# A threshold search on two engines: GpSimd answers ScalarE's count before VectorE's

## The chip, the cores and the metric

The kernel runs on one core of a Trainium2 chip. The metric is the device time of one launch in microseconds (us), where lower is better. Five engines with their own instruction queues work side by side and wait for each other through semaphores: TensorE (PE, with PEld for its weight loads), VectorE (DVE), ScalarE (ACT), GpSimd (POOL) and SyncE (SP, which only issues DMAs here).

## The reference, cut to what matters

One decoder layer is computed for a prompt of 2048 tokens and for 8 x 4 sample tokens: an input projection, a convolution branch, a sparse attention branch, and a mixture of experts. The change touches the prompt's sparse attention alone. There an indexer scores every earlier token for every query, the 256 best are kept, and attention runs over those:

```python
def indexer_select(qi, wi, kidx, qpos, k_sel):
    dots = jnp.einsum('bqhd,bsd->bqhs', qi, kidx) * (IDX_DIM ** -0.5)
    score = jnp.einsum('bqhs,bqh->bqs', jax.nn.relu(dots), wi).astype(jnp.float32)
    kpos = jnp.arange(kidx.shape[1])
    score = jnp.where(kpos[None, None, :] <= qpos[None, :, None], score, -jnp.inf)
    return lax.top_k(score, k_sel)[1]
```

The kernel does not sort. It finds for each query the score that separates the 256 best from the others, by halving an interval 25 times, and turns the result into a mask that is added before the softmax.

## The kernel before, in words

The prompt's 2048 queries are 16 tiles of 128. `attend_prompt` works through them in 64 slots `g`, four for each tile, and each slot does two of the tile's eight heads: scores on PE (L1279), mask and maximum on DVE (`masked`, L1548, then `largest`, L1555), exponential on ACT (`exp`, L1402), transposes on PE (L1296), copies of them on ACT (`keep_turned`, L1380), and the product with the values on PE (L1323). While that goes on, the indexer of eight later tiles (`SEEK`: 14, 15, 12, 13, 10, 11, 8, 9) is put between: dots on PE (L1264), relu on ACT (`keep_relu`, L1371), weighted sums over the heads on DVE (`sums`, L1482 to L1486). The longer a tile, the longer its rows, up to 2048 scores for each query.

The threshold search takes these eight tiles in four pairs. Of a pair `q`, VectorE counts the even one (`count_x`, L1499) and ScalarE the odd one (`count_y`, L1411). In each round `r` an engine reads the whole row of scores once and counts how many lie above the tile's current middle. GpSimd then moves the middle (`narrow`, L1630 to L1636) with two tiny instructions of 128x1, L1634 and L1635, and the engine may count the next round. Its waits are `mid_ready[0]` on VectorE and `mid_ready[1]` on ScalarE, and GpSimd's are `counted[0]` and `counted[1]`. So each tile's search is a chain of count, narrow, count, and GpSimd serves both chains in one fixed order.

Where the counts stand in the queues of VectorE and ScalarE is set by tables. `PACE` gives the number of rounds in a tile's four slots, and `PLACES` the places inside a slot, from 0 to 4. On VectorE (`behind`, L1592 to L1614) place 0 follows `masked(g + 1, 0)`, place 1 follows `masked(g + 1, 1)` and `largest`, places 2 and 3 follow one instruction of `sums` each in the slots that have dots (0 to 15, 24 to 31 and 36 to 43), and place 4 comes last. On ScalarE (L1438 to L1459) place 0 follows the first `keep_turned`, place 1 the second one and the first `keep_relu`, place 2 the first `exp`, place 3 the second `keep_relu` and the second `exp`, and place 4 comes last. The first search runs in slots 8 to 17 (2 or 3 rounds a slot), the second in 22 to 28 and the third in 36 to 43 (up to 5 rounds a slot), the fourth in 46 to 52 (4 rounds a slot). Since each engine's queue is in order, a count that waits for its middle holds up everything behind it.

GpSimd has little else to do here: `begin` sets up a pair, `bounds` and `finish` close it, and it issues some gathers when all searches are over.

Of the kernel before, what the change touches and what calls it, by code (L numbers as in the profile page):

```python
# [1159 lines left out]
def attend_prompt(nc, c, early, edges, kT, kiT, v_tok, wi_tok):  # L1160
# [3 lines left out]
    with Phase(nc, "q_") as ph:  # L1164
# [58 lines left out]
        with ph.block() as block:  # L1223
# [30 lines left out]
            def _(pe):  # L1254
                def dots(j, m, chunks):
                    if m == 0:
                        pe.wait_ge(qi_loaded[j % 2], 16 * (j // 2 + 1))
                    for k, (a, b) in list(enumerate(cuts(seek_length(j), 512)))[chunks]:
                        free, _, _ = at.dots[j, m, k]
                        if free:  # L1260
                            pe.wait_ge(s_free[k % 2], free)
                        for x in range(2):
                            rows = slice(x * HD, x * HD + HD)
                            nc.tensor.matmul(ps_s[k % 2][:, 512 * x:512 * x + b - a], qi_st[rows, j % 2, m, :], kiT[rows, a:b],  # L1264
                                             start=True, stop=True).then_inc(s_full[k % 2], 1)

                def scores(g, u):
                    t = g // 4
                    if g % 4 == 0 and u == 0:
                        pe.wait_ge(q_loaded[t % 2], 64 * (t // 2 + 1))  # L1270
                    a, b = cuts(length(t), 1024)[u]
                    for x in range(2):
                        free, _, _ = at.scores[g, u, x]
                        if free:
                            pe.wait_ge(s_free[x], free)
                    for k0, k1 in cuts(b - a, 512):
                        for x in range(2):
                            rows = slice(x * HD, x * HD + HD)
                            m = nc.tensor.matmul(ps_s[x][:, k0:k1], q_st[rows, t % 2, g % 4, :], kT[rows, g % 4 // 2, a + k0:a + k1], start=True, stop=True)  # L1279
                            if k1 == b - a:  # L1280
                                m.then_inc(s_full[x], 1)
# [81 lines left out]
            def _(act):  # L1363
                def keep_relu(j, m, chunks):
                    for k, (a, b) in list(enumerate(cuts(seek_length(j), 512)))[chunks]:
                        _, full, _ = at.dots[j, m, k]
                        half = at.halves[j, m, k // 2]
                        if k % 2 == 0 and half >= 2:
                            act.wait_ge(relu_used, half - 1)
                        act.wait_ge(s_full[k % 2], full)  # L1370
                        nc.scalar.activation(relu[:, half % 2, :, a % 1024:a % 1024 + b - a],  # L1371
                                             ps_s[k % 2][:].rearrange("p (x k) -> p x k", x=2)[:, :, 0:b - a], ACT.Relu, scale=IDX_SCALE).then_inc(s_free[k % 2], 1)
# [248 lines left out]
            def _(pool):  # L1621
                ch = Chain(pool, g_chain)

                def begin(j):
                    pool.wait_ge(range_ready, j + 1)
                    ch.link(nc.gpsimd.tensor_tensor(span[:, j:j + 1], most[:, j:j + 1], least[:, j:j + 1], ALU.subtract))
                    ch.link(nc.gpsimd.tensor_scalar(width[:, j % 4], pow2[:], span[:, j:j + 1], 1e-30, ALU.mult, ALU.add))
                    nc.gpsimd.tensor_tensor(mid[:, j % 4, 0:1], least[:, j:j + 1], width[:, j % 4, 0:1], ALU.add).then_inc(mid_ready[j % 2], 1)

                def narrow(j, r):  # L1630
                    q = j // 2
                    bound, compare = (TOPK - 0.5, ALU.is_ge) if j % 2 == 0 else (seek_length(j) - 2 * TOPK + 0.5, ALU.is_le)
                    pool.wait_ge(counted[j % 2], q * HALVINGS + r + 1)
                    ch.link(nc.gpsimd.tensor_scalar(step[:, j % 2:j % 2 + 1], count[:, j % 4, r:r + 1], bound, width[:, j % 4, r:r + 1], compare, ALU.mult))  # L1634
                    nc.gpsimd.tensor_scalar(mid[:, j % 4, r + 1:r + 2], mid[:, j % 4, r:r + 1], step[:, j % 2:j % 2 + 1], width[:, j % 4, r + 1:r + 2],  # L1635
                                            ALU.add, ALU.subtract).then_inc(mid_ready[j % 2], 1)  # L1636

                def bounds(j):
                    q = j // 2
                    bound, compare = (TOPK - 0.5, ALU.is_ge) if j % 2 == 0 else (seek_length(j) - 2 * TOPK + 0.5, ALU.is_le)  # L1640
                    pool.wait_ge(counted[j % 2], (q + 1) * HALVINGS)
                    ch.link(nc.gpsimd.tensor_scalar(passed[:], count[:, j % 4], bound, None, compare))
                    ch.mark(nc.gpsimd.tensor_scalar(under[:, j % 2, 0:HALVINGS], passed[:], -1.0, HUGE, ALU.add, ALU.mult))
                    ch.link(nc.gpsimd.tensor_scalar(over[:, j % 2, 0:HALVINGS], passed[:], HUGE, None, ALU.mult))
                    ch.mark(nc.gpsimd.tensor_tensor(under[:, j % 2, 0:HALVINGS], under[:, j % 2, 0:HALVINGS], mid[:, j % 4], ALU.add))
                    ch.mark(nc.gpsimd.tensor_copy(under[:, j % 2, HALVINGS:HALVINGS + 1], least[:, j:j + 1]))
                    ch.mark(nc.gpsimd.tensor_copy(over[:, j % 2, HALVINGS:HALVINGS + 1], most[:, j:j + 1]))
                    ch.link(nc.gpsimd.tensor_tensor(over[:, j % 2, 0:HALVINGS], over[:, j % 2, 0:HALVINGS], mid[:, j % 4], ALU.add))
                    pool.sem_inc(bound_ready, 1)

                def finish(j):
                    n = seek_length(j)
                    pool.wait_ge(chosen, j + 1)
                    ch.link(nc.gpsimd.tensor_tensor(sure[:, 0:n], sure[:, 0:n], edge[:, 0:n], ALU.mult))
                    nc.gpsimd.tensor_scalar(sc_row(j)[:, 0:n], sure[:, 0:n], -HUGE, 0.0, ALU.mult, ALU.add).then_inc(mask_ready, 1)
# [7 lines left out]
                for q in range(len(SEEK) // 2):  # L1663
                    for x in range(2):
                        begin(2 * q + x)
                    for r in range(HALVINGS - 1):
                        for x in range(2):
                            narrow(2 * q + x, r)
                    for x in range(2):
                        bounds(2 * q + x)  # L1670
                    for x in range(2):
                        finish(2 * q + x)
# [1960 lines left out]
```

## Time and profile before

| what | value |
|---|---|
| three runs | 2965.82, 2962.16, 2948.20 us (median 2962.16) |
| the profiled execution, its own time | 2951.22 us |
| its span from first to last instruction | 2949.5 us |
| PE, DVE, ACT, POOL busy | 2681.7, 1964.6, 1490.1, 763.5 us |
| share of the span | 91%, 67%, 51%, 26% |
| granted TensorE clock, mean over the span | 0.967 |

The busy share is an average over stages with different limits. The prompt's attention lies between about 950 and 1770 us of the span. In the page's 40 slices of some 74 us each, those are slices 13 to 23, and there DVE and ACT are both at six to nine tenths, PE at eight to nine. No engine is idle for long, and none is full, so in this stage the order in which the engines wait for one another matters. The rest of the kernel, before and after, is not touched.

Below, a group of rows gives the view it comes from. In a timeline a row reads: start in us from the span's start, duration in us, engine, line, operation, what it writes and reads, the shapes, and in brackets for how long the engine was idle before it and who ended that. A count takes two instructions, the pass over the row and a short one that reads the accumulator, and the count is over when the second ends.

### The profile page before, as it was taken

To read this page: it belongs to the slowest core of one execution; us is meant where nothing else is said; L and a number is where in the kernel's file an instruction comes from. 1 tells how busy PE (TensorE), PEld (TensorE's weight loads), DVE (VectorE), ACT (ScalarE), POOL (GpSimd) and SP (SyncE) were. 2 spreads that over 40 slices of the span, in tenths; PEclk is the share of its full clock that TensorE was granted. 3 is DMA by queue.
4 is the path that set the end of the run, shared out by engine and by line. 5 is a ranking of instruction groups with operands and counts; after the bars stand their busy time and mean duration, and the time that the engine had idled before them with its cause. 6 is when DMAs were issued, how large, how long until landed. Compare 5 with 4: busy or idle time off the path is not lost. (4 is left out here: it accounts for less than half of the span.)

```text
span 2949.5 us, 46736 instructions
## 1 busy us (share of the span) xinstructions
PE 2681.7 (91%) x16568; PEld 1712.6 (58%) x16570; DVE 1964.6 (67%) x3027; ACT 1490.1 (51%) x2535; POOL 763.5 (26%) x1012
## 2 busy tenths in 40 slices
PE   8999999999899888878878888899999599999988
PEld 6887878799898344545455565455545333333333
DVE  2499623689962788787787736574443666676658
ACT  2111123359894588687687756421000255566546
POOL 3344432233233033331333413112230000000025
PEclk9999999999999999999999999999999699999999
DMA  3322333124443221300200138644551587777857
GB/s 130 102 95 88 104 114 92 29 72 133 121 137 126 70 68 51 93 8 14 70 8 12 27 110 276 232 139 156 194 182 54 221 325 276 298 282 289 301 204 295
DMA packets 238167, 412.88 MB, mean 140 GB/s; under 512 B 29276, under 2 KB 153436, under 8 KB 229162
## 3 DMA queue, kind: packets, MB, share of 16 engines
q1 hardware_dynamic: 175122, 249.22, 25.7%
q0 software_dynamic: 24464, 86.40, 8.1%
q10 hardware_dynamic: 38416, 75.08, 7.0%
q8 instruction: 100, 1.64, 0.2%
q14 instruction: 65, 0.53, 0.1%
HBM read 317.30 MB, written 97.44 MB: 141 GB/s over the span
## 5 line engine op out<-in xcount | busy, mean ns | idle before, releaser
L471 PE MATMUL p_ps_acc<-p_x_hi,p_w_hi 128*128 128x352 f32 (+2 forms) x1480 | 529.8, 358 | 10.4 <-POOL p_w_lo L398 8.5
L471 PE MATMUL p_ps_acc<-p_x_lo,p_w_hi 128*128 128x352 f32 (+2 forms) x1480 | 520.8, 352 | 0.0
L471 PE MATMUL p_ps_acc<-p_x_hi,p_w_lo 128*128 128x352 f32 (+2 forms) x1480 | 520.1, 351 | 0.0
L471 PEld LDWEIGHTS p_ps_acc<-p_x_hi,p_w_hi 128*128 128x128 f32 (+1 forms) x1480 | 277.4, 187 | 64.4 <-issue 19.0
L471 PEld LDWEIGHTS p_ps_acc<-p_x_lo,p_w_hi 128*128 128x128 f32 (+1 forms) x1480 | 277.8, 188 | 27.8 <-issue 0.5
L471 PEld LDWEIGHTS p_ps_acc<-p_x_hi,p_w_lo 128*128 128x128 f32 (+1 forms) x1480 | 277.4, 187 | 27.3
L3230 PE MATMUL e_ps_G<-g_shared,e_xT 128*32 128x512 f32 x656 | 290.6, 596 | 1.4 <-issue 1.4
L3230 PE MATMUL e_ps_G<-g_late,e_xT 128*32 128x512 f32 x1312 | 291.4, 595 | 0.3 <-issue 0.2
L3230 PE MATMUL e_ps_G<-l_wgu,e_xT 128*32 x656 | 290.5, 596 | 1.0 <-ACT e_xT L3288 1.0
L626 ACT ACTIVATE p_stage<-p_ps_acc,g_cols 128x352 f32<-128x352 f32 (+3 forms) x145 | 88.4, 610 | 334.2 <-PE p_ps_acc L471 334.2
L396 POOL CAST p_w_hi<-g_late 128x1024 fp32r<-128x1024 f32 x74 | 92.4, 1248 | 590.3 <-PE p_ps_acc L471 447.5
L792 DVE SCALAR_TENSOR_TENSOR g_shared<-g_late,p_taps,g_shared 128x1024 f32<-128x1024 f32 x240 | 226.2, 984 | 4.2
L792 DVE SCALAR_TENSOR_TENSOR g_shared<-g_early,p_taps,g_shared 128x1024 f32<-128x1024 f32 x120 | 205.1, 1709 | 4.3
L398 POOL TENSOR_TENSOR p_w_lo<-g_late,p_w_hi 128x1024 fp32r<-128x1024 f32 x74 | 204.6, 2765 | 6.0
L1296 PE MATMUL q_ps_t<-g_ident,q_sm 128*128 128x128 f32 x1088 | 156.5, 288 | 51.9 <-ACT q_pT L1380 34.2
L1279 PE MATMUL q_ps_s<-a_keys,g_late 64*128 64x512 f32 (+3 forms) x640 | 158.2, 603 | 47.7 <-DVE q_top L1548 19.1
L1296 PEld LDWEIGHTS q_ps_t<-g_ident,q_sm 128*128 128x128 f32 x1088 | 122.4, 146 | 116.6 <-issue 63.1
L1402 ACT ACTIVATE q_sm<-q_sm,q_negmax 128x128 f32<-128x128 f32 (+15 forms) x128 | 153.4, 1199 | 56.7 <-DVE q_negmax L1555 55.8
L3230 PEld LDWEIGHTS e_ps_G<-l_wgu,e_xT 128*32 128x32 f32 x656 | 72.3, 110 | 185.8 <-issue 185.6
L1380 ACT COPY q_pT<-q_ps_t 128x512 f32<-128x512 f32 (+3 forms) x320 | 146.2, 533 | 61.0 <-PE q_ps_t L1296 60.1
L3255 PE MATMUL e_ps_Y<-l_wd,e_hT 128*32 x328 | 148.2, 594 | 21.9 <-DVE e_hT L3369 20.3
L2923 POOL DMA_INDIRECT l_rows<-x,l_slot_tok x41 | 39.0, 952 | 475.6 <-PE e_ps_X L3215 450.0
(598 smaller groups left out, 5763.3 us busy)
## 6 DMA issues: line engine op xcount, KB each, us to landing
g_late<-in_w_in_dram SPq DMA_DIRECT2D x72, 512.0 KB, 3.8
l_wgu<-in_w_gate_dram SPq DMA_DIRECT2D x32, 1024.0 KB
l_wgu<-in_w_up_dram SPq DMA_DIRECT2D x32, 1024.0 KB
l_wd<-in_w_down_dram SPq DMA_DIRECT2D x30, 1024.0 KB, 5.5
yb<-e_y ACTq DMA_DIRECT2D x41, 512.0 KB
featT<-p_stage ACTq DMA_DIRECT2D x28, 528.0 KB
featT<-p_stage ACTq DMA_DIRECT2D x28, 512.0 KB
g_late<-featT SPq DMA_DIRECT2D x56, 256.0 KB, 3.1
```

The costliest lines, as they stand in the source:

```text
L396: nc.gpsimd.tensor_copy(w_hi[:, slot], w[:, slot]).then_inc(w_hi_done, 1)
L398: nc.gpsimd.tensor_tensor(w_lo[:, slot], w[:, slot], w_hi[:, slot].bitcast(F32), ALU.subtract).then_inc(w_split[slot], 1)
L471: m = nc.tensor.matmul(acc[slot][tb][0:rows, 0:width], wp[:, slot, k, 0:rows], xp[:, k, at], start=(k == 0 and i == 0), stop=(k == KD - 1 ...
L626: nc.scalar.activation(into[0:rows, tb * width:(tb + 1) * width], acc[slot][tb][0:rows, 0:width], func, bias=c.cols[0:rows, blk:blk + 1]). ...
L792: ch.mark(nc.vector.scalar_tensor_tensor(dst, src, wt, dst, ALU.mult, ALU.add))
L1279: m = nc.tensor.matmul(ps_s[x][:, k0:k1], q_st[rows, t % 2, g % 4, :], kT[rows, g % 4 // 2, a + k0:a + k1], start=True, stop=True)
L1296: m = nc.tensor.transpose(ps_t[n % 3][:, (k - a) * P:(k - a + 1) * P], sm[:, g % 2, x, k * P:(k + 1) * P], c.ident[:])
L1380: nc.scalar.copy(pT[:, x, a:b, :], ps_t[n % 3][:, 0:(b - a) * P].rearrange("p (b q) -> p b q", q=P)).then_inc(t_kept, 1)
L1402: nc.scalar.activation(row, row, ACT.Exp, bias=negmax[:, g % 2, x:x + 1], scale=SM_SCALE, accum_out=total[:, t % 2, g % 4, x:x + 1]).then_ ...
L2923: pool.indirect_dma_start(w.rows[:, j % 2, :], None, c.x1, bass.IndirectOffsetOnAxis(ap=slot_tok[:, j:j + 1], axis=0)).then_inc(w.x_loaded ...
L3230: m = nc.tensor.matmul(pG[slot][tile_of(x), :].rearrange("p (g f) -> p g f", g=2), xT[:, k, tile_of(x)], weights, start=(k == 0), stop=(k ...
L3255: m = nc.tensor.matmul(pY[h][tile_of(x), :], hT[:, k, tile_of(x)], weights, start=(k == 0), stop=(k == 1))
```

## The change

Inside a round the two narrowings change places. Before, GpSimd waits for VectorE's count, narrows its tile, then waits for ScalarE's count and narrows that. Now it waits for ScalarE's count first. The instructions, their number, the tables, and the queues of all other engines stay as they are, and so does the order of `begin`, `bounds` and `finish`.

```diff
                 for q in range(len(SEEK) // 2):
                     for x in range(2):
                         begin(2 * q + x)
                     for r in range(HALVINGS - 1):
-                        for x in range(2):
+                        for x in (1, 0):
                             narrow(2 * q + x, r)
                     for x in range(2):
                         bounds(2 * q + x)
```

This is GpSimd's queue where the first search starts, before the change. The name in brackets is the semaphore, by an older name of its number: `p_x_loaded0` is `counted[0]` (VectorE's count is over), `p_x_loaded1` is `counted[1]` (ScalarE's), and `p_turned` is GpSimd's own chain.

```order
L1634 TENSOR_SCALAR q_step<-q_count,q_width 128x1 [waits p_x_loaded0]
L1635 TENSOR_SCALAR q_mid<-q_mid,q_step,q_width 128x1 [waits p_turned]
L1634 TENSOR_SCALAR q_step<-q_count,q_width 128x1 [waits p_x_loaded1]
L1635 TENSOR_SCALAR q_mid<-q_mid,q_step,q_width 128x1 [waits p_turned]
L1634 TENSOR_SCALAR q_step<-q_count,q_width 128x1 [waits p_x_loaded0]
L1635 TENSOR_SCALAR q_mid<-q_mid,q_step,q_width 128x1 [waits p_turned]
```

And this is the same place with the change:

```order
L1634 TENSOR_SCALAR q_step<-q_count,q_width 128x1 [waits p_x_loaded1]
L1635 TENSOR_SCALAR q_mid<-q_mid,q_step,q_width 128x1 [waits p_turned]
L1634 TENSOR_SCALAR q_step<-q_count,q_width 128x1 [waits p_x_loaded0]
L1635 TENSOR_SCALAR q_mid<-q_mid,q_step,q_width 128x1 [waits p_turned]
L1634 TENSOR_SCALAR q_step<-q_count,q_width 128x1 [waits p_x_loaded1]
L1635 TENSOR_SCALAR q_mid<-q_mid,q_step,q_width 128x1 [waits p_turned]
```

Only the semaphores have changed places; this goes on for 24 rounds in each of the four searches, 96 rounds in all. At the end of a search the last narrowing is now VectorE's, with `bounds` behind it as before:

```order
L1634 TENSOR_SCALAR q_step<-q_count,q_width 128x1 [waits p_x_loaded0]
L1635 TENSOR_SCALAR q_mid<-q_mid,q_step,q_width 128x1 [waits p_turned]
L1642 TENSOR_SCALAR q_passed<-q_count 128x25 [waits p_x_loaded0]
L1643 TENSOR_SCALAR q_under<-q_passed 128x25 [waits p_turned]
L1644 TENSOR_SCALAR q_over<-q_passed 128x25
```

## Rows read from the trace of the kernel before

**Rows 1.** Four searches: stretch, length, busy PE, PEld, DVE, ACT, POOL; clock, DMA, GB/s.

```profile
1044.00:1186.00 142.00, 119.20 (x712) 63.81 (x712) 126.93 (x155) 118.73 (x171) 49.66 (x99) 0.98 0.20 60
1227.00:1347.00 120.00, 94.92 (x672) 55.72 (x670) 99.45 (x138) 102.57 (x142) 41.89 (x100) 0.93 0.10 30
1427.00:1534.00 107.00, 86.90 (x556) 49.65 (x555) 88.32 (x136) 90.52 (x141) 41.02 (x98) 0.94 0.10 28
1575.00:1663.00 88.00, 67.53 (x582) 46.41 (x579) 61.43 (x116) 75.75 (x121) 35.79 (x111) 0.90 0.04 10
```

**Rows 2.** Waits over the whole span: us in total, times, longest one.

```profile
DVE q_edge L1499 <- POOL q_mid L1635: 35.1, 47, 1.0
ACT q_junk_act L1411 <- POOL q_mid L1635: 30.6, 23, 5.8
```

**Rows 3.** ScalarE's counts (L1411) in the first search: idle before them, until whom.

```profile
  POOL q_mid L1635: 12.8, 7
```

**Rows 4.** The same in the second search, then who waited for these counts.

```profile
  POOL q_mid L1635: 6.3, 5
...
  POOL q_step L1634: 19.2, 16
```

**Rows 5.** The same two in the third search.

```profile
  POOL q_mid L1635: 3.8, 5
...
  POOL q_step L1634: 13.9, 12
```

**Rows 6.** ScalarE's counts in the fourth search: idle before them.

```profile
  POOL q_mid L1635: 7.7, 6
```

**Rows 7.** Timeline of slot 41 (third search), places 1 to 4.

```profile
1501.96 0.20 ACT L1411 ACTIVATION_READ_ACCUMULATOR q_junk_act<-g_early,q_mid 128x1 f32 x1
1502.03 1.68 DVE L1499 TENSOR_SCALAR_CACHE_REDUCE q_edge<-g_early,q_mid 128x1408 bf16<-128x1408 f32 x1
...
1502.26 0.30 POOL L1634 TENSOR_SCALAR q_step<-q_count,q_width 128x1 f32<-128x1 f32 x1 [1.36 <-ACT q_junk_act L1411]
...
1503.64 1.28 DVE L1486 SCALAR_TENSOR_TENSOR q_sc<-g_shared,a_wi_tok,q_sc 128x1024 f32<-128x1024 f32 x1
1503.82 1.26 POOL L1634 TENSOR_SCALAR q_step<-q_count,q_width 128x1 f32<-128x1 f32 x1 [0.78 <-DVE q_edge L1499]
...
1508.30 1.68 DVE L1499 TENSOR_SCALAR_CACHE_REDUCE q_edge<-g_early,q_mid 128x1408 bf16<-128x1408 f32 x1 [0.92 <-POOL q_mid L1635]
1509.36 0.20 ACT L1411 ACTIVATION_READ_ACCUMULATOR q_junk_act<-g_early,q_mid 128x1 f32 x1
...
1510.48 1.58 ACT L1411 ACTIVATE q_junk_act<-g_early,q_mid 128x1536 bf16<-128x1536 f32 x1 [0.92 <-POOL q_mid L1635]
```

**Rows 8.** Timeline of slot 40: the relu's wait, and VectorE's wait after place 3.

```profile
1480.43 1.99 PE L1264 MATMUL q_ps_s<-a_keys,g_late 64*128 64x512 f32 x8 [1.83 <-DVE q_top L1548]
...
1481.66 1.94 ACT L1371 ACTIVATE g_shared<-q_ps_s 128x1024 f32<-128x1024 f32 x2 [2.30 <-PE q_ps_s L1264]
...
1491.66 1.23 DVE L1548 CUSTOM_DVE_ANT_0 q_sm<-q_ps_s,g_late 128x1024 f32<-128x1024 f32 x1 [0.98 <-PE q_ps_s L1279]
```

**Rows 9.** Timeline of slots 50 and 51 (fourth search).

```profile
1627.87 1.47 ACT L1402 ACTIVATE q_sm<-q_sm,q_negmax 128x1408 f32<-128x1408 f32 x1 [0.41 <-DVE q_negmax L1555]
...
1630.84 1.36 ACT L1411 ACTIVATE q_junk_act<-q_sc,q_mid 128x1280 bf16<-128x1280 f32 x1 [1.40 <-POOL q_mid L1635]
...
1639.20 0.75 DVE L1548 CUSTOM_DVE_ANT_0 q_sm<-q_ps_s,g_early,q_top 128x512 f32<-128x512 f32 x1 [1.74 <-PE q_ps_s L1279]
```

**Rows 10.** Timeline of slots 10 and 11 (first search).

```profile
1082.49 0.20 ACT L1411 ACTIVATION_READ_ACCUMULATOR q_junk_act<-q_sc,q_mid 128x1 f32 x1
...
1082.52 1.29 DVE L1486 SCALAR_TENSOR_TENSOR g_late<-g_shared,a_wi_tok,g_late 128x1024 f32<-128x1024 f32 x1
...
1084.18 2.21 DVE L1499 TENSOR_SCALAR_CACHE_REDUCE q_edge<-q_sc,q_mid 128x1920 bf16<-128x1920 f32 x1 [0.38 <-POOL q_mid L1635]
...
1096.81 2.00 ACT L1411 ACTIVATE q_junk_act<-q_sc,q_mid 128x2048 bf16<-128x2048 f32 x1 [1.99 <-POOL q_mid L1635]
```

## The prediction, made before the changed kernel had run

> **What bounds the kernel now.** I read the page first, then busy time by stretch, the waits, one line's own waits, and the timeline. The page shows the 91% of PE, but the change lies in the prompt's attention, where the four searches fill 457 us [rows 1]. There DVE is busy 127 of 142, 99 of 120, 88 of 107 and 61 of 88 us, ACT 119, 103, 91 and 76. In the first search VectorE has the least room, in the second and third both have some 15%, and in the fourth ScalarE is nearly full (76 of 88) while VectorE is not. Phases follow one another, so what this stage gains or loses goes to the end of the kernel nearly in full.
>
> The waits say how much can be won at most: VectorE waits 35.1 us for its middle (47 times, never over 1.0), ScalarE 30.6 us (23 times, up to 5.8) [rows 2]. No gain can pass 66 us, and most of VectorE's part is bare latency that the swap doesn't take away.
>
> **What a narrowing costs.** After ScalarE's count in slot 41 ends at 1502.16 (1501.96 + 0.20), its narrowing starts 0.10 later [rows 7]. VectorE's count in place 4 starts 0.92 us after the one before it ended, with nothing between but the narrowing, and so does ScalarE's [rows 7]. So a pair of instructions with its signals takes 0.92, of which some 0.88 is GpSimd's own turn (0.10 to start, 0.78 for the two). An engine that is served second, with both counts over, waits 1.80.
>
> **What the change does to a round.** It depends on which count ends last.
>
> If ScalarE ends first, before the change it waits for VectorE's count, for VectorE's narrowing and then for its own, and now it is served at once. VectorE loses nothing, since GpSimd is through by the time it asks.
>
> If VectorE ends first, before the change it is served at once, and now it waits for ScalarE's count and two narrowings. Its middle comes later by the lag of ScalarE's count plus 0.88. ScalarE gains nothing: its narrowing always came at once, since VectorE's was long over.
>
> GpSimd waited for ScalarE's count 16 times of 24 in the second search [rows 4] and 12 of 24 in the third [rows 5], so there the second case is the common one.
>
> **Second and third search: the loss.** In slot 41 VectorE counted in place 2 from 1502.03. ScalarE's count of place 1 ends at 1502.16, so now VectorE starts at 1502.16 + 1.80 = 1503.96, that is 1.9 later. Two places on, ScalarE's count of place 3 ends at 1509.56, VectorE may start at 1511.36 where it did at 1508.30: 3.1 later. These are not added up, for the lateness is measured each time against ScalarE, which goes on as before. A slot of four or five rounds thus ends some 3 us later on VectorE.
>
> Does that reach ScalarE? In slot 40 PE waited 1.83 us for VectorE's masked maximum before it did the dots, and ScalarE 2.30 us for those dots before its relu [rows 8]. The relu stands ahead of ScalarE's count of place 1. So the lateness comes back to ScalarE in the next slot, its lag behind VectorE is restored, and VectorE is made late again: it is paid per slot. The slots of this kind are 24 to 27 and 40 to 42, seven of 3 us, 21 us. Against it stands idle time of VectorE behind place 3 or 4, which takes in lateness: 0.98 us in slot 40 [rows 8], and I take as much in the slot after 27 and in one more. **Loss: 18 us.**
>
> **First search: a small loss.** VectorE is the bound here, so only its own waits count. In slot 10 ScalarE's count ends at 1082.69 while VectorE's sum L1486 runs from 1082.52 to 1083.81 [rows 10]. A GpSimd instruction that meets such a sum takes 1.26 us where it takes 0.30 alone (the one at 1503.82, beside the sum of 1503.64 [rows 7]). The odd pair then ends at about 1084.4 and the even one at 1085.3, where VectorE went on at 1084.18: 1.1 later. Of the seven rounds with sums behind, in three ScalarE waited long enough for GpSimd (1.99 us before 1096.81, for one [rows 10]) to be served early now, which costs nothing; four at some 1.0 remain, and I take half of it as covered. **Loss: 2.5 us.** ScalarE's 12.8 us of waits in this search [rows 3] go, and are worth nothing beside a full VectorE.
>
> Here a rule speaks. The Trainium skill ("SBUF — State Buffer", section "Who interferes with whom") says that a VectorE instruction with two inputs in SBUF and a GpSimd instruction that reads SBUF exclude each other, and the second to start blocks for the whole of the first. The trace agrees in one direction, with 1.26 for 0.30. With it every pair that falls on a sum costs up to 2.7 us and not 0.78; without it the first search would lose some 0.5 us and the sum below would be 2 us lower. In the other direction it would let a narrowing hold up VectorE's sum by 0.3 us at most per meeting, which would add some 5 us over the searches; no row I read shows that.
>
> **Fourth search: the gain.** There are no dots, and ScalarE is the bound. Before place 2 it waited 1.40 us for GpSimd in slot 50 [rows 9], and 7.7 us in six such waits in the search [rows 6]. These go, since ScalarE's count of place 1 ends before VectorE's there. The exponential behind feeds PE's transposes, ScalarE's copies and the next scores, for which VectorE waits 1.74 us (1639.20), and ScalarE waits only 0.41 us for VectorE's maximum [rows 9], so the whole circle gets shorter. VectorE's lateness of up to 1.3 us inside a slot falls into that 1.74. **Gain: 6.5 us.**
>
> **Elsewhere: a small gain.** In the second and third search ScalarE waited 6.3 and 3.8 us in ten waits [rows 4, 5]. Most are the bare 0.92 that stays. Two or three, in slots without dots or where ScalarE comes first, go. **Gain: 1.5 us.**
>
> Sum: 18 + 2.5 - 6.5 - 1.5 = 12.5 us slower. The profiled execution took 2951.2, so it would become 2963.7. The runs shown spread over 18 us, and their median lies 11 above the profiled execution; the mean of the four executions is 2957. I put the forecast on that: **2970 us**.
>
> **Bounds.** If each VectorE count is held back and all of it is paid, seven slots at 3.1, five further slots of the second and third search at 1, and the first and fourth search at 1 a slot for seventeen slots give 22 + 5 + 17 = 44 us, less 0. If VectorE's idle time takes in everything, only the gains remain: 8, or up to 15 were ScalarE's wait in the first search worth anything.
>
> **Rivals.**
>
> *ScalarE's freedom decides (faster, 15%).* VectorE's idle 15% in searches two and three takes in its lateness, because what it is late for (the maximum, the sums) has room behind it. For it: VectorE has 19 to 27 us idle in each of the last three searches [rows 1]. Against it: the 1.83 and 2.30 us of rows 8, which show VectorE as the one that is waited for. The place is the relu behind place 0. If it starts no later than before in slots 41 and 42, this rival holds. The time: 6.5 + 1.5 + 1 gained, 2948 beside 2957.
>
> *Nothing to be seen (20%).* The loss in searches two and three is half of mine, since the first late slot pushes VectorE behind ScalarE for good: then ScalarE comes first in later rounds and the swap costs nothing. 3 us a search for being pushed back once, 2.5 in the first search, less 8 gained: about 0, so 2957 to 2962. For it: the lateness is a shift that needn't repeat. Against it: ScalarE's lag is renewed by the relu, as above.
>
> *The full loss (10%).* All bounds at their upper end, with the sums blocked as well: 30 to 44 us, 2987 to 3001. For it: two engines at 85% leave little room, and tighter coupling passes on each delay. Against it: VectorE's idle time in slots 40 and 51.
>
> My forecast, a loss of 5 to 25 us, has 55%. That the change doesn't do what it says can't be: GpSimd's queue shows the swapped waits.
>
> **Range and chances.** 1% is 30 us, about what a measurement of this kernel tells from no change. Between a gain of 5 and a loss of 33 lie eight cases of ten: 2952 to 2990. Faster by over 1% needs nearly half of all the waits of rows 2 and has 2%; slower by over 1% is most of the last rival, 8%; within 1% has 90%.
>
> **What would show it.** In the profile after: VectorE's wait for GpSimd before its counts rises from 35.1 to some 80 us, with single waits of 2 to 4, above all from 1227 to 1347 and 1427 to 1534. ScalarE's falls from 30.6 to under 15, and what stays are waits of 0.92. GpSimd waits more for ScalarE and less for VectorE. The stretch of the fourth search gets 5 to 7 us shorter, those of the second and third some 9 us longer each, the first 1 to 4. The prediction is wrong if the second and third stretch keep their lengths, if slot 41's waits before ScalarE's relu don't grow, or if the fourth keeps its length though ScalarE's wait is gone; it would be the wrong way round if VectorE's wait stays near 35.

## The result, and the profile after

The changed kernel takes **2972.57 us** (median of 20 executions, 2963.72 to 2978.76); the kernel before, timed beside it, took 2962.97 us (20 executions, 2948.19 to 2969.44). The ratio is 1.004, with a 95% interval of 1.003 to 1.005: slower by 9.6 us between the medians and by 9 to 15 us by the interval, in a kernel that takes nearly 3000.

| | before | after |
|---|---|---|
| time of the profiled execution | 2951.22 us | 2969.33 us |
| its span | 2949.5 us | 2967.6 us |
| mean granted clock of TensorE | 0.967 | 0.961 |

The two spans lie 18.1 us apart. The attention ends 12.5 us later (the last `largest`, L1555, at 1748.85 and 1761.30); since it also starts 1.3 us earlier, it is 13.8 us longer. The other 5.6 us lie in the part behind it, which the change doesn't touch and which took 1200.6 and 1206.3 us; in other runs whose code there is the same it took between 1186 and 1208. So they say nothing of the change, and I leave them out.

**Where in the attention.** Every slot has one `largest`, so the ends of these instructions cut the attention into stretches. Stretch 26 here is the time from the end of `largest(26)` to that of `largest(27)`; it holds places 1 to 4 of slot 25 and place 0 of slot 26, since slot 25 issues the `largest` of slot 26. Where an expectation below gives lengths of slots, they are counted in this way, each by the `largest` with which it begins. So the forecast's slots 24 to 27 and 40 to 42 are stretches 25 to 28 and 41 to 43.

| from largest to largest | before | after | what runs there |
|---|---|---|---|
| 8 to 18 | 147.3 | 146.1 | first search |
| 22 to 29 | 119.8 | 131.9 | second search |
| 29 to 36 | 77.3 | 78.9 | no search |
| 36 to 45 | 135.3 | 143.4 | third search |
| 46 to 54 | 101.7 | 94.8 | fourth search |
| 54 to 63 | 81.7 | 81.7 | no search |
| 0 to 63 | 785.2 | 799.0 | all |

And one by one, where they differ most:

| stretch | 24 | 25 | 26 | 27 | 28 | 39 | 40 | 41 | 42 | 43 | 44 | 48 | 50 | 51 | 52 |
|---|---|---|---|---|---|---|---|---|---|---|---|---|---|---|---|
| before | 14.5 | 18.6 | 21.7 | 22.2 | 23.1 | 16.7 | 16.8 | 17.1 | 18.4 | 19.0 | 19.4 | 14.0 | 13.6 | 13.1 | 13.9 |
| after | 12.0 | 22.5 | 25.7 | 25.8 | 25.8 | 14.0 | 16.8 | 18.8 | 21.4 | 22.8 | 21.1 | 11.0 | 12.1 | 11.3 | 11.4 |

The waits of the whole span, after the change (who waits, for whom; us in total, times, longest one):

```profile
POOL q_step L1634 <- ACT q_junk_act L1411: 202.9, 92, 7.8
ACT q_pT L1380 <- PE q_ps_t L1296: 91.2, 65, 5.8
...
DVE q_edge L1499 <- POOL q_mid L1635: 65.7, 55, 2.7
...
POOL q_step L1634 <- DVE q_edge L1499: 43.5, 35, 4.4
...
PE q_ps_s L1279 <- DVE q_top L1548: 37.7, 23, 6.5
```

VectorE's waits for its middle rose from 35.1 to 65.7 us, and the longest from 1.0 to 2.7 [rows 2]. The row of ScalarE's waits for its middle, 30.6 us before, is no longer among the longer ones. GpSimd now waits mostly for ScalarE's count (202.9 us) and much less for VectorE's (43.5); before it was the other way round, 44.5 and 195.8. ScalarE's copies L1380 wait 91.2 us for PE's transposes, where they waited 60.1: the way by which the lateness comes back, as will be seen.

Stretches of the four searches, after (us, busy time of each engine, granted clock, DMA share, GB/s); they answer to [rows 1]:

```profile
1043.00:1184.00 141.00, 120.67 (x713) 64.52 (x710) 126.93 (x157) 120.03 (x173) 53.76 (x100) 0.96 0.20 60
1225.00:1357.00 132.00, 97.92 (x676) 58.26 (x676) 100.17 (x140) 103.19 (x142) 40.46 (x103) 0.88 0.09 27
1438.00:1552.00 114.00, 86.77 (x550) 49.62 (x549) 88.71 (x136) 90.32 (x139) 40.41 (x101) 0.92 0.09 26
1594.00:1675.00 81.00, 64.23 (x586) 46.07 (x585) 61.90 (x116) 75.68 (x122) 36.23 (x112) 0.95 0.05 11
```

VectorE does the same 99 to 100 us of work in a second stretch that is 12 us longer. The work didn't grow; the idle time did. In the fourth, ScalarE's 76 us now fill 81 and not 88.

**A late VectorE, in slot 41** (stretch 42). Timeline after, places 1 to 4; it answers to [rows 7]:

```profile
1509.12 1.67 DVE L1499 TENSOR_SCALAR_CACHE_REDUCE q_edge<-g_early,q_mid 128x1408 bf16<-128x1408 f32 x1
...
1512.74 0.20 ACT L1411 ACTIVATION_READ_ACCUMULATOR q_junk_act<-g_early,q_mid 128x1 f32 x1
...
1513.04 0.30 POOL L1634 TENSOR_SCALAR q_step<-q_count,q_width 128x1 f32<-128x1 f32 x1 [4.83 <-ACT q_junk_act L1411]
...
1514.71 1.68 DVE L1499 TENSOR_SCALAR_CACHE_REDUCE q_edge<-g_early,q_mid 128x1408 bf16<-128x1408 f32 x1 [1.93 <-POOL q_mid L1635]
...
1519.13 1.68 DVE L1499 TENSOR_SCALAR_CACHE_REDUCE q_edge<-g_early,q_mid 128x1408 bf16<-128x1408 f32 x1 [1.53 <-POOL q_mid L1635]
...
1522.02 1.68 DVE L1499 TENSOR_SCALAR_CACHE_REDUCE q_edge<-g_early,q_mid 128x1408 bf16<-128x1408 f32 x1 [1.21 <-POOL q_mid L1635]
```

VectorE's count of place 1 ends at 1510.79, but GpSimd stays with ScalarE's until 1512.94, and VectorE's next count starts at 1514.71, 1.77 us after that. I had said 1.80. From the start of place 1 to the start of place 2 it is now 5.59 us; to that of place 4, 12.90. Before the change these were 3.69 and 9.96 (from 1498.34): 1.90 and 2.94 later, where I had said 1.9 and 3.1.

**How it comes back, in slot 26.** Timeline after:

```profile
1294.83 3.21 PE L1279 MATMUL q_ps_s<-a_keys,g_late 64*128 64x512 f32 x8 [2.71 <-DVE q_top L1548]
...
1297.97 1.93 PE L1296 MATMUL q_ps_t<-g_ident,q_sm 128*128 128x128 f32 x15
...
1298.72 1.95 ACT L1380 COPY q_pT<-q_ps_t 128x512 f32<-128x512 f32 x4 [4.07 <-PE q_ps_t L1296]
...
1301.10 1.94 ACT L1371 ACTIVATE g_shared<-q_ps_s 128x1024 f32<-128x1024 f32 x2 [0.43 <-PE q_ps_s L1264]
```

PE waits 2.71 us for VectorE's masked maximum before it may write the scores of the next slot. The transposes are queued behind these scores, so ScalarE's copies wait 4.07 us. The relu, which I had named as the place, waits 0.43 us. In the kernel before, the same scores have no wait for VectorE, and the copies wait 1.49 us:

```profile
1291.78 3.04 PE L1279 MATMUL q_ps_s<-a_keys,g_late 64*128 64x512 f32 x8
...
1295.87 1.95 ACT L1380 COPY q_pT<-q_ps_t 128x512 f32<-128x512 f32 x4 [1.49 <-PE q_ps_t L1296]
```

Over the whole second search (22 to 29), ScalarE's copies waited 9.9 us for the transposes before and 24.1 us after, while its relu waited 2.1 and 1.8 us for the dots. So the lateness does return to ScalarE, but by another instruction.

**The fourth search**, slot 50 after; it answers to [rows 9]:

```profile
1643.16 1.47 ACT L1402 ACTIVATE q_sm<-q_sm,q_negmax 128x1408 f32<-128x1408 f32 x1 [0.49 <-DVE q_negmax L1555]
...
1644.63 1.35 ACT L1411 ACTIVATE q_junk_act<-q_sc,q_mid 128x1280 bf16<-128x1280 f32 x1
1645.37 1.41 DVE L1499 TENSOR_SCALAR_CACHE_REDUCE q_edge<-q_sc,q_mid 128x1152 bf16<-128x1152 f32 x1 [0.92 <-POOL q_mid L1635]
```

The count of place 2 starts when the exponential ends (1643.16 + 1.47 = 1644.63), with no wait for GpSimd; before, 1.40 us stood there. In the whole fourth search ScalarE has no such wait left, where it had 7.7 us [rows 6].

### The profile page after: what moved, and what is told of

It reads as the page before. It is cut to its first block and busy times, and to the rows that moved or that the text cites. A ratio compares the mean times of both kernels' runs of the same rounds, so it can differ in the third digit from the quotient of the medians.

```text
span 2967.6 us, 46736 instructions
## 1 busy us (share of the span) xinstructions
PE 2691.3 (91%) x16568; PEld 1721.2 (58%) x16570; DVE 1966.3 (66%) x3027; ACT 1491.0 (50%) x2535; POOL 762.9 (26%) x1012
## 5 line engine op out<-in xcount | busy, mean ns | idle before, releaser
L471 PE MATMUL p_ps_acc<-p_x_hi,p_w_hi 128*128 128x352 f32 (+2 forms) x1480 | 529.0, 357 | 10.3 <-POOL p_w_lo L398 8.3
L1380 ACT COPY q_pT<-q_ps_t 128x512 f32<-128x512 f32 (+3 forms) x320 | 147.6, 532 | 92.7 <-PE q_ps_t L1296 91.2
L3255 PE MATMUL e_ps_Y<-l_wd,e_hT 128*32 x328 | 148.2, 595 | 21.9 <-DVE e_hT L3369 20.8
```

What stands on the lines that cost most here:

```text
L471: m = nc.tensor.matmul(acc[slot][tb][0:rows, 0:width], wp[:, slot, k, 0:rows], xp[:, k, at], start=(k == 0 and i == 0), stop=(k == KD - 1 ...
L1380: nc.scalar.copy(pT[:, x, a:b, :], ps_t[n % 3][:, 0:(b - a) * P].rearrange("p (b q) -> p b q", q=P)).then_inc(t_kept, 1)
L3255: m = nc.tensor.matmul(pY[h][tile_of(x), :], hT[:, k, tile_of(x)], weights, start=(k == 0), stop=(k == 1))
```

## The experiments

In the rounds of a search, `q` is the search (0 to 3) and `r` the round. Most kernels differ from the one before only in this order, by an edit of one form. Each search and each slot can so be changed by itself. The kernel before was timed again beside each group of runs, because its median differs from group to group (2928 to 2963 us). A run of one execution says little by its time, for the kernel before spreads over some 20 us itself; there only the stretches of its profile are read.

```
-                        for x in range(2):
+                        for x in ((1, 0) if CONDITION else (0, 1)):
                             narrow(2 * q + x, r)
```

**1. The fourth search alone** (CONDITION is `q == 3`).

> ScalarE's tile is narrowed first in the fourth search alone; the other three keep VectorE first. My theory (each search pays or gains by itself, and the fourth gains because ScalarE is the bound there and comes first): the stretch from the maximum of slot 46 to that of slot 54 takes 94.8 us as with the whole change, where it took 101.7; nothing before it moves; ScalarE's waits for its middle in it (7.7 us) are gone. Time 7 us below before, ratio 0.9977. Rival (the fourth search got shorter only because the engines enter it in another position after three changed searches): the stretch keeps 101 to 102 us and the ratio is 1.000.

Measured: 2929.92 us (12 executions) beside 2938.02 (21), ratio 0.9976 (0.9960 to 0.9993). The fourth search took 95.7 us instead of 101.7. So this part of the change is a gain of some 7 us, by itself and as forecast.

The same profile has something that matters for all the rest: its third search took 141.2 us, where the profile of before has 135.3, though no round is swapped there. The row below is from the timeline of this kernel, slot 40 (in stretch 41); its counterpart is the first row of [rows 8].

```profile
1479.08 3.68 PE L1264 MATMUL q_ps_s<-a_keys,g_late 64*128 64x512 f32 x8 [1.82 <-DVE q_top L1548]
```

The same eight matmuls after the same wait (1.82 and 1.83 us) take 3.68 us here and 1.99 there. The granted clock around them, from this kernel's windows (the clock is the column before the last two):

```profile
1479.00:1482.80 3.80, 3.72 (x9) 1.38 (x10) 2.50 (x5) 1.02 (x1) 1.36 (x5) 0.55 0.00 0
```

and from those of the kernel before:

```profile
1480.40:1483.70 3.30, 3.27 (x18) 1.59 (x20) 2.44 (x5) 2.04 (x3) 1.22 (x4) 1.00 0.00 0
```

TensorE ran at its lower level (1.2 GHz) for nearly all of it here, and at its higher one (2.4) there. A single profile of before against a single one of after therefore doesn't give the price of the third search.

**2. The second search alone** (`q == 1`).

> ScalarE first in the second search alone. My theory: the stretch from slot 22 to slot 29 takes 131 to 132 us for 119.7 before, slots 25 to 28 each 2.5 to 4 us longer, slot 24 some 2.5 us shorter; all other slots as before. Rival (VectorE is pushed behind ScalarE once and then nothing more is paid): the stretch grows by 3 us, nearly all of it in the first slot that has dots, and the later ones keep their lengths.

Measured, one execution: 2953.37 us beside 2938.02. The second search took 132.4 us; stretches 24 to 28 took 12.0, 22.5, 25.7, 25.8 and 25.8, the same as with the whole change. The starts of `largest` 26 to 29:

```profile
1278.69 0.17 DVE L1555 TENSOR_SCALAR q_negmax<-q_top 128x2 f32<-128x2 f32 x1
1304.37 0.17 DVE L1555 TENSOR_SCALAR q_negmax<-q_top 128x2 f32<-128x2 f32 x1
1330.21 0.17 DVE L1555 TENSOR_SCALAR q_negmax<-q_top 128x2 f32<-128x2 f32 x1
1356.00 0.17 DVE L1555 TENSOR_SCALAR q_negmax<-q_top 128x2 f32<-128x2 f32 x1
```

Three stretches in a row take 25.7 to 25.8 us. In the kernel before:

```profile
1275.53 0.17 DVE L1555 TENSOR_SCALAR q_negmax<-q_top 128x2 f32<-128x2 f32 x1
1297.18 0.17 DVE L1555 TENSOR_SCALAR q_negmax<-q_top 128x2 f32<-128x2 f32 x1
1319.34 0.17 DVE L1555 TENSOR_SCALAR q_negmax<-q_top 128x2 f32<-128x2 f32 x1
1342.45 0.17 DVE L1555 TENSOR_SCALAR q_negmax<-q_top 128x2 f32<-128x2 f32 x1
```

Every slot loses anew: 4.0, 3.7 and 2.7 us. A shift paid once would have shown one long slot and then the old lengths. Here the rival "nothing to be seen" falls.

Is it TensorE's clock? In stretches 25 to 28 the granted clock was 1.00, 0.84, 0.92 and 0.93 before and 0.85, 0.87, 0.80 and 0.87 with the whole change. Stretch 26 begins at the full clock in both, has no lower mean with the change, and loses the most, 4.0 us. So there the loss is the order's alone. In the other three the mean is lower with the change, so part of their loss can be the clock; no run parts the two. Where the second search isn't swapped at all, it takes 118.6 to 121.2 us (runs 1 and 4), so its price of 12 us is known to some 2.

**3. One slot alone** (`q == 1 and 14 <= r <= 18`, the five rounds whose counts stand in slot 26 and whose waits fall in stretch 27).

> ScalarE first in five rounds only, 14 to 18 of the second search, which are the counts of slot 26. My theory (lateness is paid in the slot in which it arises and not again): the slots around it, 27 and at most 28, grow by 3 to 4.5 us in sum, and the engines are back in their old positions two slots later. Rival one (a shift that is paid once): the same growth as with all rounds of the search swapped, 10 to 12 us, can't come, but the growth is the same 3 us in this run and in the one with the whole second search. Rival two (VectorE's idle time takes one late slot in, and only a row of them costs): under 1 us.

Measured, one execution (2931.15 us). The same instructions:

```profile
1272.54 0.17 DVE L1555 TENSOR_SCALAR q_negmax<-q_top 128x2 f32<-128x2 f32 x1
1294.27 0.17 DVE L1555 TENSOR_SCALAR q_negmax<-q_top 128x2 f32<-128x2 f32 x1
1320.42 0.17 DVE L1555 TENSOR_SCALAR q_negmax<-q_top 128x2 f32<-128x2 f32 x1
1342.85 0.17 DVE L1555 TENSOR_SCALAR q_negmax<-q_top 128x2 f32<-128x2 f32 x1
```

Stretch 26 takes 21.7 us as before, stretch 27 takes 26.2 (+4.0) and stretch 28 takes 22.4 (-0.7). In all the second search is 3.4 us longer. One slot's rounds cost one slot's loss, and the next slot, narrowed in the old order, doesn't inherit it. (The granted clock in stretch 27 was 0.74 here and 0.92 before, so this 4.0 need not be the order's alone.) This and the run above are what shows that the loss is paid per slot. VectorE's waits in stretch 27 are those of the forecast:

```profile
1300.76 1.95 DVE L1499 TENSOR_SCALAR_CACHE_REDUCE q_edge<-g_late,q_mid 128x1664 bf16<-128x1664 f32 x1 [2.16 <-POOL q_mid L1635]
...
1305.45 1.95 DVE L1499 TENSOR_SCALAR_CACHE_REDUCE q_edge<-g_late,q_mid 128x1664 bf16<-128x1664 f32 x1 [1.54 <-POOL q_mid L1635]
...
1308.65 1.95 DVE L1499 TENSOR_SCALAR_CACHE_REDUCE q_edge<-g_late,q_mid 128x1664 bf16<-128x1664 f32 x1 [1.25 <-POOL q_mid L1635]
```

**4. The third search alone** (`q == 2`).

> ScalarE first in the third search alone. In the profiles so far that search took 135.2 or 135.3 us in two kernels that don't touch it and 139.8 to 141.2 in four others that don't either, with TensorE's granted clock in slot 41 at 0.90 in the first and 0.83 to 0.85 in the others; with the whole change it took 143.4. My theory as predicted (lateness paid per slot): slots 42, 43 and 44 grow by 2 to 3.8 us each, slot 39 gets 2.7 shorter, and the runs come out 6 to 8 us slower, ratio 1.0025. Rival (half of the difference between 135.3 and 143.4 is the clock, which falls without the change as well): slots 42 to 44 as said, but the runs only 2 to 4 us slower, ratio 1.001.

Measured: 2962.55 us (12 executions) beside 2958.13 (17), ratio 1.0014 (0.9999 to 1.0028). Its third search took 143.7 us, with stretches 39 to 44 at 14.0, 16.8, 18.8, 21.4, 22.8 and 21.2: the same as with the whole change, to 0.1 us. But the loss between the medians is some 4 us (by the interval 0 to 8), not the 8.1 that the two profiles differ by. Other profiles whose third search isn't swapped at all have 135.2 (the one slot above), 139.8 (the delayed narrowing below), 140.0 (the second search alone) and 141.2 (the fourth alone). (The 140.8 that the expectation counts with them is run 6's, which swaps three rounds there.) The 135.3 of before was one of two short ones, and against the mean of the five, 138.3, the swapped 143.4 and 143.7 are some 5 us longer. The two times don't rule out 8 by themselves; together with the profiles they speak for 4 to 5.

That these differences among equal code are TensorE's clock is read from rows; no run held the clock fixed. The mean clock of a stretch isn't enough for it: stretch 43 took 20.8 us at 0.97 in run 1 and 19.0 at 0.91 before. There the low level lies across the border of the stretch (0.50 from 1514 to 1520 in run 1, with stretch 43 from 1518.7 on; 1.00 at that place before), so PE enters the stretch behind. In run 2, unswapped there, stretch 44 has the same (0.50 from 1549 to 1553, and it begins at 1553.8): it took 19.4 or 21.2 us in swapped and in unswapped kernels alike.

**5. Only the delay, without the new order.** The pair's order stays, but in the second search GpSimd waits for both counts before it does either narrowing:

```
                     for r in range(HALVINGS - 1):
+                        if q == 1:
+                            pool.wait_ge(counted[1], q * HALVINGS + r + 1)
                         for x in range(2):
```

> The kernel before, but in the second search GpSimd waits for both counts and then narrows VectorE's tile first. It parts the two halves of what VectorE pays: waiting for the slower count, and being served second (0.88 us). My theory (both are paid, the sum is what makes VectorE late: 3.1 us at the end of a slot of five rounds, of which 0.88 is the second place): slots 26 to 28 grow by 2 to 3 us each over the kernel before instead of 3 to 4, and ScalarE's waits rise to about 1.8 us where there were 0.92 (place 3 to 4). The stretch from slot 22 to 29 takes 127 to 130 us (before 119.8, with the change 131.8), and the 2.5 us gained in slot 24 are not there. Rival (only the second place counts, since VectorE has room for the rest): the stretch stays under 123 us.

Measured, one execution (2955.49 us; the one of before beside it took 2928.08): a second search of 128.5 us, with stretches 24 to 28 at 14.1, 20.8, 23.5, 25.4 and 24.4. The loss is 8.7 where the whole swap has 12. The sum is as expected, and slot 24's gain is gone, but stretches 26 to 28 grew by 1.8, 3.2 and 1.3 where 2 to 3 each were expected. VectorE waits for the lag of ScalarE's count but not for a second narrowing, and now ScalarE three times has the bare price of being second:

```profile
1294.52 1.79 ACT L1411 ACTIVATE q_junk_act<-g_late,q_mid 128x1792 bf16<-128x1792 f32 x1 [1.80 <-POOL q_mid L1635]
```

1.80 us with both counts over: a wait of 0.92 and another engine's turn of 0.88, as worked out from [rows 7]. So waiting for the slower count, with one turn at GpSimd on top, makes most of the loss. The run doesn't part the two fully, since it moved the turn from VectorE to ScalarE.

**6. Rounds with room.** The swap only in the rounds of place 0, in front of which VectorE has idle time (`q == 1 and r in (9, 14, 19)`, `q == 2 and r in (10, 14, 19)`).

> ScalarE first only in the rounds that are counted in place 0 of slots 25 to 27 and 40 to 42 (three of the second and three of the third search). There the two counts end within 0.4 us of one another or ScalarE's first, and VectorE has 0.9 to 2.2 us between its narrowing and its next count. My theory (a round costs only what its lag plus 0.88 passes VectorE's room): nothing, slots 25 to 28 and 40 to 43 within 0.5 us of the kernel before, as long as TensorE's clock falls as it did there. Rival (every round served second costs VectorE its 0.88): some 5 us over the two searches.

Measured, one execution (2957.23 us beside 2959.44): stretches 25 to 28 took 18.6, 21.9, 23.6 and 21.8, in sum 85.9 where the kernel before has 85.6; the second search took 119.9. The third took 140.8, as in run 1 (141.2) with the same clock in stretch 41 (0.85). Stretches 27 and 28 miss the expected 0.5 us, one by +1.4 and one by -1.3, which cancel. The rival's 5 us aren't there: a late middle costs nothing where its engine isn't ready for it.

**7. PE's queue: is it the way back?** In `attend`, PE issues the scores of the next slot, which wait for VectorE, ahead of the second half of the transposes. Here it issues them behind, so that ScalarE's copies needn't wait for VectorE. One kernel does it with the whole change, one with the old order of the narrowings.

```
-                    if g + 1 < NSLOT and length(nxt) > 1024 and dotted_in(g) is not None:
-                        scores(g + 1, 1)
...
-                    if g + 1 < NSLOT and length(nxt) > 1024 and not (dotted_in(g) is not None):
+                    if g + 1 < NSLOT and length(nxt) > 1024:
                         scores(g + 1, 1)
```

> The whole change, and PE does the second part of the next slot's scores behind the second head's transposes, where in slots with dots it stood ahead of them. In the changed kernel PE waits in slots 25 to 28 for VectorE's late maximum (2.7 us) with those scores, and the transposes queue behind it, so that ScalarE waits 4 to 5.6 us for its copies. My theory (the lateness comes back through whatever needs VectorE's maximum, the dots as well as the scores): ScalarE's wait moves from the copies to the relu, slots 25 to 28 stay within 1.5 us each of the 22.5, 25.7, 25.8 and 25.8 they take with the change. Rival (the queue position of the transposes is the way back): at least half of the growth over the kernel before (3.9, 4.0, 3.6 and 2.7) goes.

> The kernel before with only that move on PE, as the control for the run before it. Both theories: slots 25 to 28 within 1 us of the kernel before (18.6, 21.7, 22.2, 23.1), since there VectorE's maximum is not late; ScalarE's copies wait a little less, its relu a little more.

Measured, one execution each: 2947.84 us with the whole change and 2958.46 with the old order (before, beside them: 2928.08). The second search took 132.0 us in **both**. With the whole change, stretches 25 to 28 took 22.4, 24.3, 24.5 and 25.4, and ScalarE's wait did move: 6.3 us for the transposes and 20.0 us for the dots over the search, where the change alone has 24.1 and 1.8. That is what my theory had said. But the control missed its expectation by far: its stretches took 20.7, 24.0, 24.9 and 24.9, and its ScalarE waits are nearly the same (4.5 and 18.9 us). The edit costs 12 us by itself, since the next slot's scores come late to VectorE, which waits 24.6 us for them where it waited 11.9 before. So the pair of runs shows nothing of the way back, which rests on the rows of slot 26 and on the waits of the search beside them. One thing it does show: where VectorE already waits elsewhere in each slot, the swap costs nothing on top in sum.

**8. An order by table.** If it is the count that ends first which should be served first, the order can be set round by round from the trace: swapped in the fourth search, in most of the first, in slot 23's first two rounds and in the third search up to slot 39 (`q == 3 or (q == 0 and r >= 2 and r != 5) or (q == 1 and r in (2, 3)) or (q == 2 and r <= 7)`).

> The order is set by round: ScalarE first in the fourth search, in the first from round 2 on but for round 5, in the second in rounds 2 and 3, in the third up to round 7; VectorE first elsewhere, so everywhere ScalarE's count comes later because of dots. My theory (serve the one that ends first): fourth search 7 us shorter, first 2.5, second 2.5 (slot 24), third 2 (slot 39); in all 14 us less than before, ratio 0.995. Rival (the gains in slots 24 and 39 only borrowed from the slots after them, whose losses give them back): 8 to 9 us, the second and third search unchanged in sum.

Measured: 2924.52 us (10 executions) beside 2938.02 (21), **ratio 0.9954 (0.9939 to 0.9968)**: 13.5 us faster than before, and the best of all kernels here. Its four searches took 145.9, 116.5, 133.3 and 94.9 us, all from 0 to 63 together 770.0. That is 15.2 less than before, but 5.0 of it lie in 54 to 63, where there is no search. The losing stretches 25 to 28 are back at 19.0, 20.9, 21.7 and 23.2. Stretches 24 and 39 keep their gains (12.0 and 14.0), and those behind them don't give them back, as the rival would have it. Some of the 116.5 is clock again: stretch 26 took 20.9 here and 21.7 before, in the same order.

A finer table, without rounds 2 and 5 of the third search and with two changes more in the first and fourth (`(q == 3 and r > 0) or (q == 0 and r >= 2) or (q == 1 and r in (2, 3)) or (q == 2 and r <= 7 and r not in (2, 5))`):

> The table of the earlier run, mended by what its trace showed: ScalarE first also in round 5 of the first search, and VectorE first in round 0 of the fourth and in rounds 2 and 5 of the third, where ScalarE's count came later. My theory: 1 to 2 us less than with the first table, in slots 10 to 13 and 38; ratio to before 0.995, which this measurement can't tell from the first table. Rival (the position the engines reach matters more than the single round): a sum as before or worse by up to 2 us.

Measured: 2948.05 us (8 executions) beside 2959.44 (11), ratio 0.9957 (0.9936 to 0.9979), with searches of 146.4, 119.5, 137.9 and 95.9. The two tables can't be told apart by their times, and the 1 to 2 us expected aren't in the profile either: stretches 10 to 13 took 61.8 us for the first table's 61.4, and 38 took 11.5 for 11.6. Stretch 39 took 16.3 us where the first table has 14.0, and unswapped kernels 16.7 to 17.0; one of the two rounds taken out, 5, falls in it (the clock was 0.79 here and 1.00 there, so not all of the 2.3 need be the order). So serving the count that had ended first in that round's trace did not gain there.

## Why the prediction was right, point by point

The time lies in the range, its sign and sum are right: +12.5 us forecast, 9.6 between the medians. The range alone would prove little, since the 2962.97 us of the kernel before lie in it too; what counts is the sign, clear of noise, and the terms. That 2970 came within 3 us of 2972.57 is in part luck: the kernel before turned out 6 us slower than the 2957 that I had started from, and the loss 3 us smaller. The +12.5 at the attention's end in the profile is luck as well, for the profile of before had a favourable clock in the third search. By terms it is less neat, and errors cancel: the second and third search lost 20.2 us in the profiles, where I had 18 less a gain of 1.5, and the first gained 1.2 where I had a loss of 2.5.

- **The price of a narrowing and of being second: right.** 0.92 and 1.80 were forecast; 0.92, 1.77 and 1.80 stand in the rows above.
- **Lateness inside a slot: right.** 3.1 forecast and 2.94 measured at place 4 of slot 41; 1.9 and 1.9 at place 2.
- **Paid per slot: right, by another way.** I said that PE's dots, and by them the relu, wait. In the trace it is PE's scores of the next slot with the transposes queued behind them, and ScalarE's copies that wait. My own sign of being wrong, "if slot 41's waits before ScalarE's relu don't grow", came true (0.72 us before and after) and meant nothing, since it named the wrong instruction. Runs 2 and 3 show the payment per slot; the way itself is read from slot 26 and no run isolates it.
- **Second search: right, with two errors that cancel.** Its losing slots were the four that I had named, but they lost 3.9, 4.0, 3.6 and 2.7 (stretches 25 to 28, 14.2 us) where I had 12 less what idle time takes in. Against it stands a gain of 2.5 in stretch 24, where ScalarE comes first. In run 1, in the old order but at full clock, that stretch took 12.9, before 14.5 at a clock of 0.88, after 12.0 at 1.00: so 0.9 of the gain is the new order, and the rest goes with the clock.
- **Third search: the slots right, the size too high.** Stretches 41 to 43 lost 1.7, 3.0 and 3.8. Stretch 44 lost 1.7, unforecast, but takes as long in runs 2 and 5, where it isn't swapped either. Stretch 39 gained 2.8. My share was some 8, and the two profiles differ by 8.1. But the timed runs give 4, with an interval from 0 to 8, and the other profiles 5. Nearly half of what looks like a confirmation is that the profile of before had a favourable clock there.
- **"Elsewhere", a gain of 1.5: too small.** It was meant for slots of these two searches where ScalarE comes first, and stretches 24 and 39 gained 2.5 and 2.8, of which 24's is partly clock. My reading of ScalarE's ten waits there, mostly the bare 0.92, was wrong: four of them were (0.88 to 0.95), and of the 10.1 us 5.4 stayed.
- **First search: wrong in sign**, +2.5 forecast and -1.2 measured. I held ScalarE's times fixed and asked only when VectorE is served. But ScalarE, served early, runs 1 to 3 us ahead and feeds PE earlier, and VectorE's waits for PE's scores in stretches 14 and 16 (0.90 us at 1136.51 and 0.94 at 1166.81 before) vanish, and each is 1.0 shorter. Only stretch 9, with rounds 0 and 1, lost the 1.3 of my reasoning. The step that failed is "ScalarE's waits in this search are worth nothing beside a full VectorE".
- **The Trainium skill's rule ("SBUF — State Buffer", section "Who interferes with whom")**: in the first search VectorE waited 9.0 us for GpSimd before and 11.0 after, 15 times in both. Thirteen waits kept their lengths; two grew, from 0.39 to 1.70 (before 1057.73) and from 0.38 to 1.14 (before 1084.41), and in front of both a narrowing meets a VectorE sum and takes 1.20 and 1.30 us instead of some 0.3 or 0.4. So the trace agrees with the rule, and most of the 2 us that I had set aside did appear; only two rounds had them, and not four, and the gains in stretches 14 and 16 outweigh them. No wait of a sum for a narrowing can be read from these rows.
- **Fourth search: right.** -6.5 forecast, -6.9 in the profile, and 2938.02 to 2929.92 in run 1. Of the 3.0 us of stretch 48 only 1.4 is ScalarE's wait; the rest goes with its clock (0.77 before, 1.00 after).
- **The waits.** VectorE's 65.7 us against "some 80"; the single waits of 2 to 4 reach only 2.7. ScalarE's fell to 6.2, under 15 as said: none are left in the fourth search, 0.7, 3.0 and 2.4 us in the first three.

By parts: the first -1 and the second +12 by the profiles, the third +4 and the fourth -8 by the timed runs (the fourth -7 by the profile), in sum +7 to +8; measured were 9.6, and the interval of that begins at 9.

Of the rivals, "nothing to be seen" falls by runs 2 and 3. "ScalarE's freedom decides" was right for the first search and the fourth, and wrong where a search runs beside dots with five rounds a slot. "The full loss" needed every late count to be paid, which run 6 contradicts.

What stays open: how much of the second search's gain in the table kernel is order and how much clock, how much of the loss in stretches 25, 27 and 28, and whether the transposes behind the scores are the only way back. It was read in the second search; in the third the copies' waits rose from 8.8 to 18.1 us, and in run 1, unswapped, they were 11.7.

## What to carry to other kernels

Where one engine serves two in turn, serving first the one whose work ends last can cost time in every stage, and which that is can change from stage to stage: read it from who the server waits for, and set the order by table. The finer table shows the limit of such a reading, for serving a round the other way moves the rounds behind it. Being served second costs the lag of the other's work plus the server's turn, less the idle time in front of the next use; in a loop whose stages hand work to each other each slot can pay it anew. Before two single profiles are compared stage by stage, look at the stages that the change doesn't touch: here they moved by up to 7 us, as much as some that it does.

## What the runs showed of the hardware

Stages of equal code differ by up to 7 us between executions: the third search, unswapped, took 135.2 to 141.2 us, and the stretches 54 to 63, which have no search, 76.0 to 83.1. Much of the first goes with TensorE's granted clock. Stretch 41 took 17.1 us at 0.90 and 19.6 at 0.85; stretch 35, without any search, took 8.6 to 8.8 us with the clock at 1.00 (the kernel before and run 3) and 10.3 to 10.7 at 0.84 or 0.85 in all others. In run 1 the lower level followed a wait of PE of 1.82 us, and in the kernel before a wait of 1.83 us at the same place was followed by the full clock. What decides between the two isn't shown.

Most of the second isn't the clock. Stretch 57 took 7.5 to 7.8 us in seven kernels and 11.9 to 13.0 in five. In the kernel before, where it took 13.0, PE was busy for 0.76 of the 2.00 us from 1702 to 1704 with the clock at 1.00, and its transposes there stand apart with no wait that the profile names, while the DMA share was 1.01. Run 1 has DMA shares of 0.95 to 1.03 in the same stretch and takes 7.8 us. What holds PE up there isn't shown.
